# Decode rows between the two prompt tiles of a projection chunk, in a two-layer inference step on one core

## What is computed

```
def even_layer(...):                      # layer 0; layer 1 is built likewise
    z = rmsnorm(x, pre_w) @ w_in          # 3652 columns; layer 1: 6924
    qa, ka, va, ga, qb, kb, vb, gb, qi, ki, wi = split_cols(z, EVEN_SPLITS)
    qa = rope(qa, pos) ...                # rotary on q, k of each branch
    oa = diff_attention(qa, ka_all, va_all, pos, lam, lam_init)
    ob = dsa_attention(qb, qi, wi, ki_all, fetch_k, fetch_v, pos)
    mix = concat([oa * silu(ga), ob * silu(gb)])
    y = x + rmsnorm(mix @ w_out, post_w)
```

## Time and profile before

| what | value |
|---|---|
| median of the runs | 836.67 us (835.9, 836.67, 841.24) |
| span of the profiled execution, first to last instruction | 829.1 us |
| around the span, against the median | 7.6 us |
| PE busy | 758.0 us (91%) |
| DVE busy | 433.8 us (52%) |
| ACT busy | 247.6 us (30%) |
| PE idle (829.1 less 758.0) | 71.1 us |
| HBM traffic over the span | 327 GB/s |

### The profile page before, as it was taken

How to read it: one execution, slowest core, us unless ns; L and a number is a source line. 1 busy time by engine, 2 the same in 40 slices (tenths; PEclk the granted TensorE clock), 3 DMA queues, 4 the chain that set the end, 5 groups by cost and what they waited for, 6 DMA issues and landing times.

```text
span 829.1 us, 13098 instructions
## 1 busy us (share of the span) xinstructions
PE 758.0 (91%) x5032; PEld 412.9 (50%) x5032; DVE 433.8 (52%) x981; ACT 247.6 (30%) x617; POOL 167.9 (20%) x204
## 2 busy tenths in 40 slices
PE   6889999989998799998999997999999999999896
PEld 4455545444454334443455654555565455554443
DVE  2214588889966989746253243324655345331214
ACT  5334233233213301122154323333320232242222
POOL 0333312012330333430101022402140001101000
PEclk9999999999999999999999999999999999999899
DMA  8656767789795777696695394885689658955911
GB/s 282 210 197 233 278 221 291 298 305 367 272 340 165 254 275 275 238 334 260 222 316 198 123 392 166 308 339 191 241 310 400 241 191 318 378 195 179 363 57 53
DMA packets 68357, 213.01 MB, mean 257 GB/s; under 512 B 5072, under 2 KB 28800, under 8 KB 62920
## 3 DMA queue, kind: packets, MB, share of 16 engines
q0 software_dynamic: 20864, 142.55, 46.6%
q1 hardware_dynamic: 47272, 69.53, 24.0%
q10 hardware_dynamic: 160, 0.11, 0.0%
HBM read 206.14 MB, written 64.68 MB: 327 GB/s over the span
## 4 chain that ended last, share of the span: by engine, by line
PE 70%; DVE 11%; DMA 7%; ACT 6%; issue 4%; another core or an unknown queue 1%; POOL 1%; DVEq 0%; ACTq 0%; SPq 0%
PE psum L910 30%; PE psum L976 9%; PE psum L839 8%; PE psum L921 5%; PE psum L891 4%; DMA ring<-in_w_in_odd 4%; PE psum L1031 2%; PE psum L1065 2%; DMA ring<-in_cache_a_v,index 2%; DVE SA L2382 2%; PE psum L1318 2%; PE psum L1161 1%; ACT Z L1488 1%; DVE ring L2380 1%; PE psum L1243 1%
## 5 line engine op out<-in xcount | busy, mean ns | idle before, releaser
L910 PE MATMUL psum<-ring,XB 128*128 128x512 f32 (+3 forms) x712 | 301.5, 575 | 1.6 <-issue 1.0
L910 PEld LDWEIGHTS psum<-ring,XB 128*128 128x128 f32 x712 | 131.9, 191 | 141.9 <-issue 137.7
L976 PE MATMUL psum<-Z,ring 128*128 128x512 f32 x256 | 116.4, 599 | 1.9 <-issue 1.3
L1940 DVE TENSOR_TENSOR RT<-Z,const 128x128 f32<-128x128 f32 (+6 forms) x43 | 11.5, 267 | 129.5 <-ACT Z L1578 108.0
L976 PEld LDWEIGHTS psum<-Z,ring 128*128 128x128 f32 x256 | 46.4, 189 | 60.1 <-issue 59.9
L1578 ACT ACTIVATE Z<-psum,stat 128x512 f32<-128x512 f32 (+3 forms) x38 | 24.2, 637 | 167.7 <-PE psum L910 153.0
L891 PE MATMUL psum<-ring,XB 128*128 128x512 f32 (+1 forms) x120 | 56.6, 620 | 2.6 <-DMA ring<-in_w_in_even 1.5
L921 PE MATMUL psum<-ring,XB 128*8 128x128 f32 (+3 forms) x1664 | 49.6, 267 | 3.8 <-issue 2.4
L921 PEld LDWEIGHTS psum<-ring,XB 128*8 128x8 f32 x1664 | 41.4, 90 | 22.0 <-issue 21.1
L1740 ACT ACTIVATE SM<-SM,stat 128x128 f32<-128x128 f32 (+4 forms) x56 | 27.0, 482 | 76.7 <-DVE stat L2127 75.6
L1488 ACT COPY NW<-psum 128x512 f32<-128x512 f32 (+1 forms) x56 | 32.8, 585 | 48.5 <-PE psum L839 46.7
(11 more groups left out here) (350 smaller groups left out, 943.1 us busy)
## 6 DMA issues: line engine op xcount, KB each, us to landing
ring<-in_w_in_odd SPq DMA_DIRECT2D x9, 2048.0 KB, 15.2
ring<-in_w_in_even SPq DMA_DIRECT2D x6, 2048.0 KB
ring<-in_cmp_w SPq DMA_DIRECT2D x4, 2048.0 KB
ring<-in_w_in_odd SPq DMA_DIRECT2D x8, 1024.0 KB
out_s_d_k<-in_state_d_k POOLq DMA_DIRECT2D x8, 1022.0 KB
out_s_d_v<-in_state_d_v POOLq DMA_DIRECT2D x8, 1022.0 KB
Z<-in_cmp_w POOLq DMA_DIRECT2D x5, 1024.0 KB, 7.7
ring<-in_w_out_even SPq DMA_DIRECT2D x2, 2048.0 KB
```

Source lines behind the costliest of these rows:

```text
L910: last = mm(out[:, 0:n], xT[:, k, t * 128:(t + 1) * 128], w[:, k * n:(k + 1) * n], start=k == 0, stop=k == KT - 1)
L976: last = mm(out[:, h * 512:(h + 1) * 512], w[:, (r % 16) * CH + h * 128:(r % 16) * CH + h * 128 + 128], rowsT[:, at:at + 512], start=r == ...
```

## The change

In chunks that are not gated, `decode_rows(l, i)` moves from behind `rows(l, i, 1)` to behind `rows(l, i, 0)`, on every engine. Gated chunks and chunk 0 of each layer keep their order. The second tile is now the last reader of the weights, so `rows` names the release; in gated chunks `decode_rows` still names it after that. `spare_from` is set by the second tile of chunk 12.

```diff
@@ even_order
         order.append(("rows", 0, i, t))
-        if t and i:
+        if i and t == (i in GATED[0]):
             order.append(("decode_rows", 0, i))
@@ odd_order
             order.append(("rows", 1, i, t))
-            if t and i:
+            if i and t == (i in GATED[1]):
                 order.append(("decode_rows", 1, i))
@@ build
-        spare_from = step_of["decode_rows", 1, LAST[1] - 1]
+        spare_from = step_of["rows", 1, LAST[1] - 1, 1]
@@ rows, on PE
                 copied[l, i, t] = (P.filling, P.made)
+                if t:
+                    release(f"win{l}_{i}", P.full, P.made)
```

## The result

The changed kernel takes 849.88 us (median of 4 runs, 849.22 to 852.82) against 837.76 us before (median of 4): 1.4% slower, ratio 1.0143, 95% interval [1.0092, 1.0194]. The forecast was 837.5 us.

What follows compares the result with a forecast made beforehand. PE was taken to set the time (busy 758.0 of 829.1 us), so only its waits could change; the terms summed to +0.8 us on 836.67, forecast 837.5 us, likely 835.5 to 839.5, outer ends 830.5 to 843.5.

Steps and rivals of the forecast that it cites:

- Chunk 1 of layer 0, -3.0: Moved block fills a PE wait before the second tile and leaves the stretch behind it: -3.0 us (-3.85 to -1.7).
- the stall and the late chain: Layer 0 chunk 1: block stands for instruction issue, 4.0 us instead of 1.9; PE waits 1.81 us behind ACT's late small work.
- Chunk 2, +0.4: Layer 0, between first and second tile: a row of transposes bound by ACT gets longer, +0.4 us (0 to +0.5).
- chunks 4 and 5, -0.5: Layer 0, behind the second tiles: waits for ACT shorten, partly offset by DVE's earlier rotary work; -0.5 us for both (-1.0 to 0).
- Layer 1, chunks 2, 4 and 5, +1.6: PE waits longer between the tiles, on ACT and DVE at chunk 2, DVE at chunk 4: +1.0, +0.45 and +0.15 us.
- Chunk 6, +2.2: Layer 1: DVE's decode softmax chain starts later and the block no longer covers it, +2.2 us (0 to +3.9).
- Chunks 8 and 10, 0: Layer 1: no change, since their waits start and end in the same stretch between tiles; 0 us.
- SP's loads start when they did. POOL's order stays: Weights are released at the second tile's end, when the block ended before, so SP's load starts and POOL's order are unchanged.
- Chunk 12, +0.3: Layer 1: PE's wait behind a DVE and ACT chain, first part 1.9 us later, less the block's 1.13; +0.3 us (0 to +0.5).
- The base: The profiled execution lies 7.6 us under the 836.67 us median, taken as time around the span that does not change.
- The clock (0.09): Rival, chance 0.09: longer waits at layer 1's chunks 2, 4, 6, 12 each drop PE's clock, 1.7 us apiece; 844.3 or 845.6 us.
- The gain at the start doesn't come: Rival, chance 0.20: the stalls at layer 0's chunk 1 only move to an open place; +1.3 us, 838.8 us.

Runs made afterwards that it cites:

- l0_only: The kernel before with only the decode blocks of layer 0's chunks 1 to 5 moved, layer 1 as before; ratio 0.9992 against the kernel before.
- l0_third_only: The kernel before with only the decode block of layer 0's chunk 3 moved; ratio 0.9998 against the kernel before.
- changed_again: The changed kernel itself, run again on the chip of the experiments; ratio 1.0112 against the kernel before, +9.2 us.
- order_before: Control with no decode block moved, the same instruction lists as the kernel before; ratio 0.9966 against it.
- l1_first_four: The kernel before with only the decode blocks of layer 1's chunks 1, 2, 4 and 5 moved; ratio 1.0024 against the kernel before.
- l1_only: The kernel before with only the ten decode blocks of layer 1 moved, layer 0 as before; ratio 1.0143 against the kernel before.

## Why the prediction was wrong

Three of its steps failed: the loads of chunks 10 and 12 come late, for which it had no term (3.0 us of waits); the term of chunk 6, +2.2, measured 5.0; and the gain of 3.0 us at chunk 1 is not there in the runs. Step by step:

- **Chunk 1 of layer 0, -3.0.** The mechanism held in the first pair of traces: -4.4 (1.2 of them the clock's) against -3.85 to -1.7. It failed as a term. The waits behind the second tile gave 1.8 us back at once, and on five chips, where the stall and the late chain are missing, the move of chunk 1 costs 0.3 us in the trace of l0_only and the five moves of layer 0 are worth 0 (0.9992 and 1.0019). I took a stall whose cause the trace does not show as a property of the order. The same order lacks it on five chips.
- **Chunk 2, +0.4; chunks 4 and 5, -0.5.** In l0_only against l0_third_only the steps are +0.4, 0.0 and -0.1: B wins 0.37 us each time, but A pays 0.4 and 0.2.
- **Layer 1, chunks 2, 4 and 5, +1.6.** Right: changed_again against order_before has +1.1, +0.4 and +0.05, and l1_first_four costs 2.0 us.
- **Chunk 6, +2.2.** Right as a wait (3.09 against 0.90 us). As a time it is 5.0 us (2.2 to 7.8): the term was mis-sized by the clock that falls behind it in some executions. I had the fall in its upper end (+3.9) and held against it that the clock was full behind a wait of 0.90 us; with 1.3 and 1.75 us close together it was not.
- **Chunks 8 and 10, 0.** Wrong. At chunk 8 the transposed mask (VCp) waits 1.33 us in place of 0.87, +0.45. At chunk 10 the step that failed is "SP's loads start when they did. POOL's order stays": both are true, and it does not follow that the loads land when they did. POOL's transfers, released in stretch A, start 1.8 us later against SP's. That is 1.0 us at chunk 10 and 2.0 us at chunk 12 that no term and no end of my range held. There was a sign of it before: PE already waited 0.60 us for the weights of chunk 9 (3.15 in order_before), so the loads there had no slack.
- **Chunk 12, +0.3.** Right (+0.3).
- **The sum.** The terms, as steps from order_before's trace to changed_again's: 1.1 + 0.4 + 0.05 + 2.4 + 0.45 - 0.35 (chunk 9) + 1.0 + 2.0 + 0.3 = +7.4 us of waits, where my terms of layer 1 gave +3.9. The mean granted clock of the runs, 0.9768 against 0.9824, is worth an estimated 0.0056 x 830 = 4.6 us more. That makes 12.0, but the wait of 3.15 us for the weights of chunk 9 is still to come off: order_before has it and changed_again has not, since PE came there late anyway, so that it hides a part of what was lost ahead of it. With it the sum is 8.9, and this kernel's runs gave 9.2. In l1_only's trace that wait stands (3.52 us), and its runs gave 11.8, as the first pair gave 12.1. So the size of the loss depends on whether this wait is there, and both sums lie within the runs' intervals of some 4 us either way.
- **The base.** The prediction took 7.6 us as lying around the span and unchanged. Some 2 us lie there; for the rest, the traced execution lay under the median. The forecast of a difference does not hang on it.
- **The rivals.** The clock (0.09) was half right: its price came, but as a mean over executions (an estimated 4.6 us) and not as four certain falls of 1.7, and it needed the waits for transfers beside it to reach +12. Its own two times, 844.3 and 845.6, lay outside the range that I gave. "The gain at the start doesn't come" (0.20) was true of layer 0 on five chips, without its 838.8. The range ended at 843.5 because all its ends were terms of waits I had seen; a resource at its limit (transfers late in layer 1, share 1.00 from 610 to 650 us in order_before) had no term.

## What to carry to other kernels

When an order of instructions changes, look at every queue that is released from within the stretch that is put off, and not only at the loads that feed the moved work: where transfers run at full share, a load that starts 2 us later can make another queue's load late. Cover over a wait can be worth more than its length when a second wait lies close behind it, since the clock may fall. And a stall with no releaser is no gain to be counted before the same order has shown it on a second chip.

## What was not expected of the hardware

- Chips differ at one place: on five, the same order has no stall in its first 100 us and takes 825 to 828 us; where before takes 836 to 838, PE's sequence of 64 small matmuls (decode rows) is broken by stalls of 0.3 to 1.1 us without a releaser, and PE is 10.3 us later by the scores of chunk 3 (91.23 against 80.97). The stalls are only a part of that: in the trace of before all of PE's "issue" time at decode rows is 2.4 us. Chunk 3's broken block (80.4 to 88.7 us) lies where POOL is issuing gathers of cache_b_idx (76.8 to 86.6 us in the trace of after). That the gathers cause them is a guess; it wasn't tried. The Trainium skill ("Runtime: NRT & Kernel Launch", section on instruction fetch mechanics) holds fetch to be sequential, in blocks of 256 instructions, and hidden by the rate of issue. If these stalls are fetch, the 8.3 us block speaks against the second. And the count does not decide alone, as it does in the prediction: five chips have no stall at the same count. No run here shows that they are fetch.
- The fall of the clock behind two waits of 1.3 and 1.75 us is no certain thing: three executions of seven had it. It shows in the means of runs and can be absent from any one trace.
